# High halves and squares of five residual stages on ScalarE, and another order of ScalarE's work in an input projection

## The reference

```python
# first block, cut
u = rms_norm(h, norm_mix_g); proj = u @ w_in            # Hyena and mLSTM branches, mixed
h = h + mixed @ w_out                                    # residual 0
h = h + cross_attention(rms_norm(h, norm_x_g), ...)      # residual 1, projection wo
h = h + square(relu(rms_norm(h, norm_ff_g) @ ff_w1)) @ ff_w2   # residual 2
x = rms_norm(h, final_norm_g)
# second block, cut
proj = rms_norm(x, ln1_g) @ w_in                         # b_a, c_a, x_a, x_b, g_b, two gates
y_a = b_a * causal_conv(c_a * x_a)
u_b = causal_conv(x_b) + b
r = sigmoid(u_b @ w_a + b_a); i = sigmoid(u_b @ w_x + b_x)
a = exp(-c * r * softplus(-lam)); b = sqrt(1 - a**2) * (i * u_b)
y_b = scan(h_t = a_t * h_(t-1) + b_t) * gelu(g_b)
merged = sigmoid(ga) * (y_a @ w_out_a) + sigmoid(gb) * (y_b @ w_out_b)
x = x + merged @ w_o                                     # residual 3
h = rms_norm(x, ln2_g)
x = x + (silu(h @ w_gate) * (h @ w_up)) @ w_down         # residual 4
return rms_norm(x, final_g)
```

## Time and profile before

| | |
|---|---|
| median of 3 runs | 1944.73 us (1944.62 to 1947.07) |
| profiled execution | 1949.02 us, span 1947.2 us |
| granted PE clock, mean | 0.956 |
| PE busy | 1776.1 us |
| VectorE busy | 1055.6 us |
| ScalarE busy | 584.5 us |
| GpSimd busy | 753.2 us |

### The profile page before, as it was taken

One profiled execution on the slowest core, in us unless ns is written; L12 is line 12 of the kernel. 1 busy time (PEld: TensorE's weight loads), 2 busy tenths in 40 slices (PEclk: granted clock), 3 DMA queues, 4 the chain that ended last, 5 costly groups with the idle time before them and its releaser, 6 DMA issues.

```text
span 1947.2 us, 21967 instructions
## 1 busy us (share of the span) xinstructions
PE 1776.1 (91%) x7718; PEld 1433.0 (74%) x7718; DVE 1055.6 (54%) x1379; ACT 584.5 (30%) x709; POOL 753.2 (39%) x312
## 2 busy tenths in 40 slices
PE   6799988975889998999999789898999999999996
PEld 4677876654667677888888577676888888888885
DVE  5751487879782566233248867575533463133137
ACT  2322332332212221111111254646433233122221
POOL 3432441113333143444444244444544444444442
PEclk9899998987899998999999899999999999999998
DMA  4232220110222022222222122223222222222222
GB/s 156 87 109 76 96 78 33 44 44 32 87 97 76 33 92 71 97 97 97 97 97 97 65 87 93 102 86 104 91 97 97 97 95 96 94 95 96 97 97 97
DMA packets 47694, 169.28 MB, mean 87 GB/s; under 512 B 5204, under 2 KB 5204, under 8 KB 47320
## 3 DMA queue, kind: packets, MB, share of 16 engines
q1 hardware_dynamic: 44640, 160.45, 23.6%
q10 hardware_dynamic: 3000, 8.09, 1.2%
HBM read 166.43 MB, written 2.10 MB: 87 GB/s over the span
## 4 chain that ended last, share of the span: by engine, by line
issue 31%; PE 29%; POOL 13%; DVE 1%; POOLq 0%; ACT 0%; DVEq 0%
POOL m_w_lo L433 13%; PE ps L465 10%; PE ps L467 10%; PE ps L466 10%; DVE m_h L1917 0%; DVE m_s L1187 0%; POOLq L441 0%; POOLq L439 0%; POOL m_QL L453 0%; DVE m_qs L1559 0%; PE ps L493 0%; DVE m_qs L1561 0%; DVE m_s L1894 0%; DVE m_ftmp L1551 0%; DVE m_ftmp L1549 0%
## 5 line engine op out<-in xcount | busy, mean ns | idle before, releaser
L433 POOL TENSOR_TENSOR m_w_lo<-m_raw,m_w_hi 128x1024 fp32r<-128x1024 f32 x302 | 738.8, 2450 | 1119.1 <-ACT m_w_hi L875 1119.1
L875 ACT ACTIVATE m_w_hi<-m_raw 128x1024 fp32r<-128x1024 f32 x302 | 317.7, 1056 | 761.4 <-DMA m_raw<-in_strips 757.6
L465 PE MATMUL ps<-m_XH,m_w_hi 128*128 128x512 f32 x1160 | 474.4, 409 | 36.6 <-POOL m_w_lo L433 22.5
L466 PE MATMUL ps<-m_XL,m_w_hi 128*128 128x512 f32 x1160 | 458.8, 396 | 0.0
L467 PE MATMUL ps<-m_XH,m_w_lo 128*128 128x512 f32 x1160 | 458.6, 395 | 0.0
L465 PEld LDWEIGHTS ps<-m_XH,m_w_hi 128*128 128x128 f32 x1160 | 222.7, 192 | 101.0 <-POOL m_w_lo L433 27.2
L466 PEld LDWEIGHTS ps<-m_XL,m_w_hi 128*128 128x128 f32 x1160 | 223.0, 192 | 47.6 <-issue 2.7
L467 PEld LDWEIGHTS ps<-m_XH,m_w_lo 128*128 128x128 f32 x1160 | 222.0, 191 | 47.9
L465 PE MATMUL ps<-m_FH,m_w_hi 128*128 128x512 f32 x432 | 168.9, 391 | 3.3 <-DVE m_FL L1180 3.2
L466 PE MATMUL ps<-m_FL,m_w_hi 128*128 128x512 f32 x432 | 168.6, 390 | 0.0
L467 PE MATMUL ps<-m_FH,m_w_lo 128*128 128x512 f32 x432 | 168.5, 390 | 0.0
(11 more groups left out here) (311 smaller groups left out, 2295.8 us busy)
## 6 DMA issues: line engine op xcount, KB each, us to landing
m_raw<-in_strips SPq DMA_DIRECT2D x302, 512.0 KB, 3.2
m_x_in<-in_x ACTq DMA_DIRECT2D x8, 256.0 KB, 4.6
m_x_res<-in_x ACTq DMA_DIRECT2D x1, 2048.0 KB, 8.0
out<-m_h SPq DMA_DIRECT2D x8, 256.0 KB, 2.1
m_memf<-in_mem ACTq DMA_DIRECT2D x1, 1024.0 KB, 10.4
m_decay<-in_decay ACTq DMA_DIRECT2D x1, 1024.0 KB, 15.1
m_w<-in_w ACTq DMA_DIRECT2D x1, 512.0 KB, 13.6
m_skip<-in_skip ACTq DMA_DIRECT2D x1, 512.0 KB, 3.9
```

Source lines behind the costliest of these rows:

```text
L433: nc.gpsimd.tensor_tensor(w_lo[:, c], raw[:, c], f(w_hi[:, c]), ALU.subtract).then_inc(lo_ready, 1)
L465: pe.matmul(dst, w_hi[:, c], xh, start=first, stop=False)
L466: pe.matmul(dst, w_hi[:, c], xl, start=False, stop=False)
L875: act.activation(w_hi[:, c], raw[:, c], ACT.Copy).then_inc(hi_ready, 1)
```

## The change

In the residual stages ScalarE gets two instructions for each tile: the high half (a copy with the gain as scale, `x_high`) and the square (`squared`), in a new function `tiles_out`, which also does the strips' high halves, one ahead of each tile. VectorE keeps the addition, the low half and the sum of squares (`summed`); its loops over tiles are unrolled, and the first tile's square is copied instead of added to a cleared `acc`. In the third stage ScalarE also squares h times `fin_g` to `e1`, for the second sum. The squares go to `s0` and `s1` in turn; ScalarE waits for the sum of two tiles before. In the last stage there is only the square, and VectorE sums one tile late. The last two pieces of the diff are the third and the last stage on VectorE, in place of their loops. In the input projection gelu goes from ahead of the sigmoids to behind the square root, and `ahead(n+5)` from behind the square to ahead of the exp.

```diff
+            def tiles_out(r, s, e, gain, dh, first=0, second=None):
+                for u in range(KT):
+                    if u >= first and s + u + 3 < N_STRIPS:
+                        ahead(s + u)
+                    act.wait_ge(evac, e + u + 1)
+                    if dh is not None:
+                        act.activation(tile(dh, u), tile(h, u), ACT.Copy, scale=gain(u)).then_inc(x_high, 1)
+                    if u >= 2:
+                        act.wait_ge(summed, 8 * r + u - 1)
+                    act.activation((s0, s1)[u % 2][:], tile(h, u), ACT.Square).then_inc(squared, 1)
+                    if second is not None:
+                        if u:
+                            act.wait_ge(summed_two, u)
+                        act.activation(e1[:], tile(h, u), ACT.Square, scale=second(u)).then_inc(squared_two, 1)
...
-            for u in range(1, N_SQ):
-                ahead(S_WOUT + u)
+            tiles_out(0, S_WOUT, E_WOUT, lambda k: col("x_g", k), YH, first=1)
...
-            squares(S_XO, N_SQ // 4)
+            tiles_out(1, S_XO, E_XO, lambda k: col("ff_g", k), YH)
...
-            squares(S_FF, N_FF // 4)
+            squares(S_FF, N_FF // 4 - 2)
+            act.wait_ge(gain_two, 1)
+            tiles_out(2, S_FF + 56, E_FF + 56, lambda k: misc[:, k:k + 1], XH, second=lambda k: col("fin_g", k))
...
                 ahead(n + 4)
-                act.wait_ge(in_free[4], mt + 1)
-                act.activation(t2[5][:], t2[4][:], ACT.Gelu_apprx_tanh).then_inc(gelu_out, 1)
                 act.wait_ge(pe_done, n + 6)
                 act.activation(t2[6][:], ps[:, 5, :], ACT.Sigmoid, bias=col("ba", mt)).then_inc(achain, 1)
                 act.activation(t2[7][:], ps[:, 6, :], ACT.Sigmoid, bias=col("bx", mt)).then_inc(gates_free, 1)
+                ahead(n + 5)
                 act.wait_ge(gates_free, mt + 1)
                 act.activation(t2[8][:], t2[6][:], ACT.Exp, scale=misc[:, 56 + mt:57 + mt]).then_inc(lru_a, 1)
                 act.activation(t2[10][:], t2[6][:], ACT.Tanh, scale=misc[:, 48 + mt:49 + mt]).then_inc(achain, 1)
                 act.wait_ge(lru_a, mt + 1)
                 act.activation(a_sq[:], t2[8][:], ACT.Square).then_inc(lru_e, 1)
-                ahead(n + 5)
                 act.wait_ge(lru_q, mt + 1)
                 act.activation(l_root[:], s0[:], ACT.Sqrt).then_inc(lru_r, 1)
+                act.wait_ge(in_free[4], mt + 1)
+                act.activation(t2[5][:], t2[4][:], ACT.Gelu_apprx_tanh).then_inc(gelu_out, 1)
...
-            squares(S_WO2, N_SQ // 4)
+            tiles_out(3, S_WO2, E_WO2, lambda k: col("ln2_g", k), XH)
...
-                    for u in range(8):
-                        ahead(s + u)
+                    tiles_out(4, s, e - 8, None, None)
...
+            def add_square(r, u):
+                dve.wait_ge(squared, 8 * r + u + 1)
+                x = (s0, s1)[u % 2]
+                if u:
+                    dve.wait_ge(summed, 8 * r + u)
+                    dve.tensor_tensor(acc[:], acc[:], x[:], ALU.add).then_inc(summed, 1)
+                else:
+                    dve.tensor_copy(acc[:], x[:]).then_inc(summed, 1)
+
+            def residual(r, first_s, first_e, gain, dh, dl, src=h):
+                ch.sync()
+                for u in range(KT):
+                    dve.wait_ge(pe_done, first_s + u + 1)
+                    dve.tensor_tensor(tile(h, u), tile(src, u), ps[:, u % 4, :], ALU.add).then_inc(evac, 1)
+                    dve.wait_ge(evac, first_e + u + 1)
+                    dve.wait_ge(x_high, 8 * r + u + 1)
+                    dve.scalar_tensor_tensor(tile(dl, u), tile(h, u), gain(u), f(tile(dh, u)), ALU.mult, ALU.subtract
+                                             ).then_inc(x_ready, 1)
+                    add_square(r, u)
+                dve.wait_ge(summed, 8 * r + KT)
                 dve.sem_inc(norm_sum, 1)
...
+            for u in range(KT):
+                n = 48 + 8 + u
+                dve.wait_ge(pe_done, S_FF + n + 1)
+                dve.tensor_tensor(tile(h, u), tile(h, u), ps[:, u % 4, :], ALU.add).then_inc(evac, 1)
+                dve.wait_ge(evac, E_FF + n + 1)
+                dve.wait_ge(x_high, 16 + u + 1)
+                dve.scalar_tensor_tensor(tile(XL, u), tile(h, u), misc[:, u:u + 1], f(tile(XH, u)),
+                                         ALU.mult, ALU.subtract).then_inc(x_ready, 1)
+                add_square(2, u)
+                dve.wait_ge(squared_two, u + 1)
+                if u:
+                    dve.wait_ge(summed_two, u)
+                    dve.tensor_tensor(e0[:], e0[:], e1[:], ALU.add).then_inc(summed_two, 1)
+                else:
+                    dve.tensor_copy(e0[:], e1[:]).then_inc(summed_two, 1)
...
+                    for u in range(KT):
+                        dve.wait_ge(pe_done, s + u + 1)
+                        dve.tensor_tensor(tile(h, u), tile(h, u), ps[:, u % 4, :], ALU.add).then_inc(evac, 1)
+                        if u:
+                            add_square(4, u - 1)
+                    add_square(4, KT - 1)
```

More of the change, by code:

```diff
@@ L309, in build @@
         x_ready = sem("x_ready")
+        x_high = sem("x_high")
+        squared = sem("squared")
+        summed = sem("summed")
+        gain_two = sem("gain_two")
+        squared_two = sem("squared_two")
+        summed_two = sem("summed_two")
         conv = sem("conv")
@@ L1624, in _ @@
                         ch.add(ins)
-            def residual(first_s, first_e, gain, dh, dl, src=h):
-                ch.sync()
[L1630 to L1642, removed]
+            def add_square(r, u):
[7 more added lines that the diff above has]
+            def residual(r, first_s, first_e, gain, dh, dl, src=h):
+                ch.sync()
+                for u in range(KT):
[7 more added lines that the diff above has]
+                dve.wait_ge(summed, 8 * r + KT)
                 dve.sem_inc(norm_sum, 1)
             dve.wait_ge(ld_h, 16)
-            residual(S_WOUT, E_WOUT, "x_g", YH, YL, x_res)
+            residual(0, S_WOUT, E_WOUT, lambda k: col("x_g", k), YH, YL, x_res)
             norm(2)
@@ L1699, in _ @@
             outputs_pair(3)
-            residual(S_XO, E_XO, "ff_g", YH, YL)
+            residual(1, S_XO, E_XO, lambda k: col("ff_g", k), YH, YL)
             norm(3)
@@ L1737, in _ @@
             ch.sync()
+            dve.sem_inc(gain_two, 1)
             def hidden_chunk(c):
@@ L1760, in _ @@
             hidden_chunk(3)
[L1764 to L1780 removed]
+            for u in range(KT):
[13 more added lines that the diff above has]
+                    dve.tensor_copy(e0[:], e1[:]).then_inc(summed_two, 1)
+            dve.wait_ge(summed, 16 + KT)
+            dve.wait_ge(summed_two, KT)
             dve.sem_inc(norm_sum, 1)
@@ L1878, in _ @@
                 dve.sem_inc(mg_ready, 1)
-            residual(S_WO2, E_WO2, "ln2_g", XH, XL)
+            residual(3, S_WO2, E_WO2, lambda k: col("ln2_g", k), XH, XL)
             norm(5, 6)
@@ L1900, in _ @@
                 last = size == FFN_CHUNKS[-1]
-                if last:
-                    ch.add(dve.memset(acc[:], 0.0))
-                with ch.loop(2, 8 if last else 0) as i:
-                    for u in range(4):
-                        hm = h[:, bass.ds(i * (4 * T) + u * T, T)]
-                        dve.wait_ge(pe_done, i * 4 + (s + u + 1))
-                        dve.tensor_tensor(hm, hm, ps[:, u, :], ALU.add).then_inc(evac, 1)
-                        if last:
-                            dve.wait_ge(evac, i * 4 + (e + u + 1))
-                            ch.sync()
-                            add_squares(hm)
+                if not last:
+                    with dve.Fori(0, 2) as i:
+                        for u in range(4):
+                            hm = h[:, bass.ds(i * (4 * T) + u * T, T)]
+                            dve.wait_ge(pe_done, i * 4 + (s + u + 1))
+                            dve.tensor_tensor(hm, hm, ps[:, u, :], ALU.add).then_inc(evac, 1)
+                else:
+                    for u in range(KT):
[4 more added lines that the diff above has]
+                    add_square(4, KT - 1)
                 s, e = s + 8, e + 8
-            ch.sync()
+            dve.wait_ge(summed, 32 + KT)
             dve.sem_inc(norm_sum, 1)
```

17 lines of the change are left out of this document (removed).

## The result

The changed kernel took 1900.05 us (median of 4 runs, 1897.95 to 1900.95), the kernel before 1944.67 us beside it (4 runs, 1944.56 to 1947.07). The ratio is 0.9766, 95% interval [0.9749, 0.9783]: 44.6 us faster by the medians, 45.5 by the ratio, which is formed from the single runs and not from the two medians. 1901 had been forecast.

The account below looks back on a forecast made before the run. PE, busy 91%, gains only where it stands still; the turns are bound by a VectorE and ScalarE chain. 9.5 + 15.8 + 1.9 + 16.6 = 43.8 us, so 1944.73 - 43.8 = 1901 us; range 1889 to 1918.

Parts of the forecast that it names:

- First residual stage: End of the first residual stage, at the Q projection: PE's waits for YL end and the norm matmul gets cheaper, 9.5 us.
- The waits' part: First residual stage: the norm matmul follows one undisturbed strip of 5.44 us after the Q projection's start, gain 8.26 us.
- The norm part: First residual stage: the norm matmul costs 0.86 us instead of 2.11, gain 1.25 us.
- the catch-up fails: Rival, first residual stage: VectorE doesn't catch up with PE; some 30 us gained in all, within 1915 to 1918; shared chance 0.10.
- End of the first feed-forward: Input projection's first strip: no wait up to the norm matmul, 15.8 us, and the second sum ready earlier, 1.9 us.
- The turn: Input projection: gelu leaves the VectorE and ScalarE chain and the scan runs free, 2.15 us a turn, 16.6 for eight.
- The moved high half: Input projection: the high half of strip n+8, moved earlier, ends PE's longest wait, but PE had that time to spare.
- The other stages: XO, WO2 and the end of the FFN: nothing is late there, gain 0; last stage between -0.3 and +0.5 us.
- The order at the way to SBUF: Rival, turns: VectorE's last low half goes ahead of GpSimd's, 1.4 us more a turn, 11 in all, 1890; chance 0.12.
- Gelu late: Rival, turns: gelu comes 1.4 us late and holds its product, 0.75 us a turn instead of 2.15, 1912; chance 0.13.
- the third: Rival: the turns give nothing, or VectorE's catch-up fails in the first stage; 27 or some 30 gained, 1915 to 1918; 0.10.
- Lockstep: Rival, residual stages: a tile's round over three engines takes 7.9 us, exceeding 5.44; some 22 us slower, 1967; chance 0.04.

Follow-up runs that it names:

- e1: The changed kernel with the turns of the input projection in their old order: 1919.44 us, ratio 0.9846 to the kernel before.
- e2: The kernel before with only the new order of the turns, residual stages as before: 1931.06 us, ratio 0.9906.
- e3: The kernel before with only gelu moved behind the square root in the turns: 1933.37 us, ratio 0.9918.
- e7: The changed kernel with the decay's square made by VectorE instead of ScalarE: 1896.88 us, ratio 0.9743 to the kernel before.
- e8: The changed kernel with both sigmoids computed as tanh of half the argument, one table load less a turn: 1893.10 us, ratio 0.9718 to the kernel before.
- e6: The changed kernel with two extra 128x512 copies between the square root and gelu's table load: 1911.63 us, ratio 0.9811 to the kernel before.
- e4: The kernel before with only the next strip's high half moved ahead of exp in the turns: 1944.32 us, ratio 0.9976.
- e5: The changed kernel with the old loops in XO, WO2 and the end of the FFN: 1904.62 us, ratio 0.9779 to the kernel before.
- e9: The changed kernel with sigmoids as tanh and the decay's square on VectorE: 1891.84 us, ratio 0.9726 to the kernel before.

## Why the prediction was right

**The bound.** It was said that the edits can touch three places where PE stands still, that two of them are the ends of residual stages with VectorE late, and that the third isn't PE's at all but a chain over VectorE and ScalarE. e1 and e2 separate them, and e3, e7 and e8 confirm the chain: what is removed from ScalarE's part (1.94, 0.63, 1.28) comes back in the distance of the turns as 1.95, 0.50 and 1.23.

**First residual stage, 9.5 forecast.** The waits' part came out as 8.26 to the hundredth, because it is a difference between a measured stretch and an undisturbed strip, and needs only that the lateness ends. That the measured stretch was a typical one was luck: from the profile of e3, where the same code took 11.70, the same working would have given 6.26. The norm part gave 1.25 for 1.25, and it is a matter of the clock: the prediction named slower matmuls behind the waits without saying what made them slower, and the matmuls it took as the norm's cost were at half rate before and aren't now. What was wrong is how early VectorE catches up: tile 5 or 6 had been said, and it was the last. The walk had put the end of tile 4 at 24 us behind the first; it came after 18.8 (534.90 to 553.67), and still VectorE was 5.4 us late for tile 5. VectorE's timeline of the changed kernel:

```profile
550.79 2.88 DVE L1655 TENSOR_TENSOR m_acc<-m_acc,m_s 128x512 f32<-128x512 f32 x1
553.60 0.68 DVE L1664 TENSOR_TENSOR m_h<-m_x_res,ps 128x512 f32<-128x512 f32 x1
555.13 0.75 DVE L1667 SCALAR_TENSOR_TENSOR m_YL<-m_h,m_const,m_YH 128x512 fp32r<-128x512 f32 x1 [0.86 <-ACT m_YH L912]
...
556.40 0.68 DVE L1664 TENSOR_TENSOR m_h<-m_x_res,ps 128x512 f32<-128x512 f32 x1
557.95 1.59 DVE L1667 SCALAR_TENSOR_TENSOR m_YL<-m_h,m_const,m_YH 128x512 fp32r<-128x512 f32 x1 [0.86 <-ACT m_YH L912]
559.46 2.88 DVE L1655 TENSOR_TENSOR m_acc<-m_acc,m_s 128x512 f32<-128x512 f32 x1
562.27 0.68 DVE L1664 TENSOR_TENSOR m_h<-m_x_res,ps 128x512 f32<-128x512 f32 x1
...
565.07 0.68 DVE L1664 TENSOR_TENSOR m_h<-m_x_res,ps 128x512 f32<-128x512 f32 x1
566.62 1.59 DVE L1667 SCALAR_TENSOR_TENSOR m_YL<-m_h,m_const,m_YH 128x512 fp32r<-128x512 f32 x1 [0.86 <-ACT m_YH L912]
```

From tile 2 to tile 7 the tiles come in pairs: one is hit in both SBUF operations (1.59 and 2.88), the next in none, and two tiles take 562.27 - 553.60 = 8.67 us, 4.3 each. Against PE's 5.44 that gains 1.1 a tile. Tile 7's addition still comes about 3 us after PE (its strip's end lies one strip before 564.55, at 559.11), tile 8's half a us. The last one's low half is ready at 568.21, and PE reads it after seven eighths of the strip, at 564.55 + 4.76 = 569.31: a reserve of 1.1 us, and 0.8 to 1.1 in all nine profiles with the new first stage; in each the stretch is 5.44. The forecast of "no wait" held by this much, so the rival "the catch-up fails" was near. (Its sum was off: without the 9.5 of this stage 34.3 are left, 1910, and not "some 30".)

**End of the first feed-forward, 15.8 and 1.9 forecast.** 15.79 and 1.92. ScalarE's timeline there:

```profile
1055.06 0.73 ACT L912 ACTIVATE m_XH<-m_h,m_misc 128x512 fp32r<-128x512 f32 x1 [1.73 <-DVE m_h L1796]
1055.69 0.62 ACT L915 ACTIVATE m_s<-m_h 128x512 f32<-128x512 f32 x1
1056.21 0.71 ACT L919 ACTIVATE m_e<-m_h,m_const 128x512 f32<-128x512 f32 x1
```

and VectorE's:

```profile
1057.16 0.68 DVE L1805 TENSOR_TENSOR m_e<-m_e,m_e 128x512 f32<-128x512 f32 x1
...
1061.57 0.69 DVE L1815 SCALAR_TENSOR_TENSOR m_acc<-ps,m_s 128x512 f32<-128x512 f32 x1 [0.24 <-PE ps L831]
```

0.73, 0.62 and 0.71 on ScalarE, where 0.75, 0.63 and 0.75 had been allowed. The second sum is done at 1057.84, 3.7 us after the strip's end at 1054.14 (3.8 forecast). No operation is hit here, and the part for the second sum begins 1061.57 - 1059.58 = 1.99 after the norm matmul (1.95 forecast, 3.89 before).

**The turn, 2.15 forecast, 2.35 measured.** ScalarE in one turn of the changed kernel, as the earlier trace rows of before:

```profile
1186.78 0.61 ACT L1159 ACTIVATE m_a_sq<-m_t 128x512 f32<-128x512 f32 x1
1187.41 1.28 ACT L1161 ACT_TABLE_LOAD   x1
1188.71 0.63 ACT L1161 ACTIVATE m_l_root<-m_s 128x512 f32<-128x512 f32 x1
1189.36 1.28 ACT L1163 ACT_TABLE_LOAD   x1
1190.65 0.63 ACT L1163 ACTIVATE m_t<-m_t 128x512 f32<-128x512 f32 x1
1191.19 1.04 ACT L881 ACTIVATE m_w_hi<-m_raw 128x1024 fp32r<-128x1024 f32 x1
```

VectorE beside it:

```profile
1189.37 0.69 DVE L1875 TENSOR_TENSOR m_t<-m_t,m_l_root 128x512 f32<-128x512 f32 x1 [1.25 <-ACT m_l_root L1161]
1190.10 1.22 DVE L1877 TENSOR_TENSOR_SCAN m_s<-m_t,m_t 128x512 f32<-128x512 f32 x1
1191.39 0.69 DVE L1880 TENSOR_TENSOR m_t<-m_s,m_t 128x512 f32<-128x512 f32 x1
1192.11 0.43 DVE L1200 TENSOR_SCALAR m_BH<-m_t 128x512 fp32r<-128x512 f32 x1
1192.58 2.76 DVE L1202 SCALAR_TENSOR_TENSOR m_BL<-m_t,m_BH 128x512 fp32r<-128x512 f32 x1
1195.43 0.69 DVE L1834 TENSOR_TENSOR m_pX<-ps,m_rstd 128x512 f32<-128x512 f32 x1
```

and GpSimd's low half:

```profile
1192.31 2.48 POOL L439 TENSOR_TENSOR m_w_lo<-m_raw,m_w_hi 128x1024 fp32r<-128x1024 f32 x1 [5.62 <-ACT m_w_hi L881]
```

Each step is as forecast: gelu is ready at 1191.28, the scan at 1191.32, 0.04 apart; the low half falls on VectorE's last one (2.76) instead of the scan. The size is off by 0.2, by one step: from the start of the strip's high half to the start of its low half I had put 1.30 us (1194.85 to 1196.15), although show 1.12 (1194.83 to 1195.95), and it is 1.12 now (1191.19 to 1192.31). So the low half starts 2.94 after the product with the root and not 3.15. That carries through to the next turn: 6.06 after the product instead of 6.25. With 1.12 the same walk would have given 2.33.

By the Trainium skill (ScalarE: Activation LUTs, "What ACT_TABLE_LOAD costs") a drain of about 1.38 us belongs to each switch of tables. The trace doesn't agree: load and gelu follow the root without one (1188.71, 1189.36, 1190.65), and e6, which put 1.30 us there, cost 8.8 us that the changed kernel doesn't show.

**The moved high half.** The prediction said that it ends PE's longest wait and that PE had that time to spare. That holds: e4 leaves 20.4 of 22.5 us of waits, in pieces of at most 1.5. Its share in the turn wasn't stated: the walk took the product with the root as undisturbed and didn't say that the moved high half makes it so. So I expected next to nothing of e4, and it is 0.53 a turn alone and 31.49 - 31.09 = 0.40 beside gelu, of which the product makes 0.34 (1.03 in e3, 0.69 in the changed kernel).

**The other stages, 0 forecast.** e5 agrees within its interval. The last stage gives 0.3 us, by the wait of the final norm matmul; between -0.3 and +0.5 had been said.

**The rivals.** The order at the way to SBUF (1890) didn't turn: the turn's last low half on VectorE was held in the first seven turns (2.75 to 2.76 us); in the last one, where no low half of GpSimd meets it, it took 0.69. Gelu late (1912) is what e6 made; that its median is 1911.63 is in part chance, since the kernel before ran 3 us slower beside it, and its turns gave back 1.17 and not 1.4. The turns gave 17.9, so the third is out. Lockstep (1967) is out too, but not because no round exceeded 5.44: in the first stage the rounds from one addition to the next are 2.65, 7.39, 2.80, 5.86, 2.80, 5.87 and 2.80 us. Each long one is followed by a short one, and such a pair averages 4.3. At the feed-forward's end they are PE's 5.44.

What stays open: why the first YH matmul comes at 560.7 to 567.5 us in different executions. The four profiles with the old first stage lie from 564.68 to 567.50 (mean 565.7), the nine with the new one from 560.70 to 566.35 (mean 564.0). They overlap, so whether the change has a small part in it can't be said, and no run was made on it. It is larger than several terms of the sum. The same holds of the stretch of 485 us, whose two groups touch at 485.23: a share of the change in it can be neither shown nor excluded, and e1's 3 us over its forecast are left open with it.

## What to carry to other kernels

When an engine's waits name a producer that isn't busy itself, look one level further: here PE waited for GpSimd's low halves, but the distance of the turns was set by a chain over two other engines, and the gain was the length of the instruction that stood on that chain without being needed there (gelu, 1.95 of 1.94 us). Place such an instruction beside the partner's long operation, and check that it fits: 0.04 us was enough, 1.3 more cost 1.17 at once. Moves on such a ring also shift which operation meets GpSimd, so walk the new order with the low half's start before adding two savings: 0.50 and 1.23 together gave 1.22 (1.31 without the first turn). And compare two profiles over short stretches from a common point on: the first 560 us differed by up to 5.7 us between executions of the same code.

## What the runs showed of the hardware

**Gelu's table serves tanh.** In e8 the tanhs of turns two to eight follow gelu of the turn before with no load between (first load of the turn only before the exp, 1180.67); the first turn, which no gelu precedes, has a load before its tanhs and none before the exp. A turn got shorter by the load's length, 1.23 of 1.28 us.

**VectorE with two SBUF operands and GpSimd exclude each other, both ways.** VectorE's last low half took 2.76 us instead of 0.69 beside a low half of 1192.31 to 1194.79, and GpSimd's low half of e4 took 3.12 instead of 2.4 where the scan had begun first. In e3 an operation with one SBUF operand was held too (the high half `BH`, 2.56 instead of 0.43). By the Trainium skill (SBUF — State Buffer, "SBUF: two separate sides") the one that starts first holds the shared ports for its whole instruction and the other is blocked; the rows agree. They show in addition that the waiting one gets its turn next: with low halves back to back (e9, two from 1174.79) VectorE's operation of 1175.89 was over at 1177.74, between the two, and the pair took 5.22 us, where two free ones take 4.8.

**PE's clock fell where PE waited long.** At the end of the feed-forward the granted clock was 0.70 and 0.50 in two stretches in which PE was busy for 1.53 of 8.0 and 2.75 of 7.6 us, and the norm matmuls behind took 2.08 us instead of 1.02.
